# Expert blocks of a mixture of experts: 32x32 squares turned by VectorE in place of full transposes by TensorE

## What is computed

```python
D_MODEL = 1024
N_EXPERTS = 32
TOP_K = 2
D_EXPERT = 512
...
    def run_block(args):
        tok, gate, e = args
        xb = x_pad[tok]
        hdn = jax.nn.silu(xb @ wg[e]) * (xb @ wu[e])
        return (hdn @ wd[e]) * gate[:, None]
```

## Time and profile before

| | |
|---|---|
| median of 3 runs | 3002.2 us (2997.6 to 3004.9) |
| the profiled execution, first to last instruction | 3002.4 us |
| mean granted clock of TensorE in it | 0.969 of 2.4 GHz |
| TensorE busy | 2798.6 us (93%) |
| VectorE, ScalarE, GpSimd busy | 1423.0, 888.2, 416.7 us |
| bytes moved by DMA | 580.55 MB, mean 193 GB/s |
| loops over blocks (experts) | from about 2036 us to 2913 us |

### The profile page before, as it was taken

The page is one execution under the profiler, slowest core; times in us unless marked ns, Lnnn a source line. Parts: engine busy times, 40 slices in busy tenths (PEclk is TensorE's granted clock), DMA queues, the critical chain, the costliest instruction groups (busy, mean ns, idle before and its releaser), DMA issues. The chain is left out here.

```text
span 3002.4 us, 81057 instructions
## 1 busy us (share of the span) xinstructions
PE 2798.6 (93%) x33765; PEld 1640.7 (55%) x33766; DVE 1423.0 (47%) x3553; ACT 888.2 (30%) x1898; POOL 416.7 (14%) x633
## 2 busy tenths in 40 slices
PE   6998999999999989999998799958999999999988
PEld 3432445455454557887787455524555555555543
DVE  3246356555566647777777344561222222222218
ACT  2347244344344434444444122210000000000006
POOL 0000000000000001121123000003222222222223
PEclk8999999999999989999999799979999999999999
DMA  8641124223232396556553785555896588768858
GB/s 296 217 142 43 50 86 136 74 106 119 99 127 107 119 252 162 161 156 183 160 151 90 242 295 196 218 202 183 302 336 252 202 303 310 282 247 297 293 198 341
DMA packets 377451, 580.55 MB, mean 193 GB/s; under 512 B 56526, under 2 KB 240774, under 8 KB 374184
## 3 DMA queue, kind: packets, MB, share of 16 engines
q1 hardware_dynamic: 327176, 486.12, 47.2%
q0 software_dynamic: 18832, 70.53, 6.7%
q10 hardware_dynamic: 31248, 21.08, 2.4%
HBM read 412.03 MB, written 165.60 MB: 192 GB/s over the span
## 5 line engine op out<-in xcount | busy, mean ns | idle before, releaser
L523 PE MATMUL pj_P<-normed,pj_wc 128*128 128x448 f32 (+2 forms) x1600 | 594.8, 519 | 0.9 <-ACT pj_stage L656 0.9
L2714 PE MATMUL moe_PG<-wgu,moe_xT 128*32 128x256 f32 x9600 | 550.7, 381 | 0.0
L523 PEld LDWEIGHTS pj_P<-normed,pj_wc 128*128 128x128 f32 x1600 | 295.8, 190 | 259.5 <-issue 243.6
L2714 PEld LDWEIGHTS moe_PG<-wgu,moe_xT 128*32 128x32 f32 x9600 | 297.0, 110 | 206.6 <-issue 26.8
L2544 DVE TENSOR_TENSOR moe_sg<-moe_sg,moe_PG 128x128 f32<-128x128 f32 x150 | 43.1, 288 | 556.0 <-ACT moe_sg L2593 556.0
L2725 PE MATMUL moe_PTY<-wd,moe_hT 128*32 128x256 f32 x4800 | 286.5, 379 | 0.6 <-DVE moe_hT L2549 0.6
L2593 ACT ACTIVATE moe_sg<-moe_PG 128x128 f32<-128x128 f32 x150 | 41.8, 278 | 793.3 <-PE moe_PG L2714 793.3
L2132 PE MATMUL merge_PO<-merge_w,merge_mT 128*128 128x512 f32 x544 | 240.0, 599 | 0.6 <-ACT merge_mT L2178 0.6
L2725 PEld LDWEIGHTS moe_PTY<-wd,moe_hT 128*32 128x32 f32 x4800 | 155.9, 110 | 103.5 <-DVE moe_y L2537 0.7
L2132 PEld LDWEIGHTS merge_PO<-merge_w,merge_mT 128*128 128x128 f32 x544 | 102.7, 191 | 125.1 <-issue 124.4
L2636 POOL DMA_INDIRECT moe_xg<-scratch_h,moe_row x154 | 149.9, 974 | 125.7 <-POOL moe_xc L2649 114.9
(11 more groups left out here) (434 smaller groups left out, 4231.6 us busy)
## 6 DMA issues: line engine op xcount, KB each, us to landing
wgu<-in_w_gate SPq DMA_DIRECT2D x32, 2048.0 KB
wgu<-in_w_up SPq DMA_DIRECT2D x32, 2048.0 KB
wd<-in_w_down SPq DMA_DIRECT2D x32, 2048.0 KB
scratch_y_rows<-merge_zeros SPq DMA_DIRECT2D x51, 512.0 KB, 4.8
scratch_hk<-pj_hk SPq DMA_DIRECT2D x16, 1344.0 KB, 5.8
normed<-scratch_hk SPq DMA_DIRECT2D x32, 640.0 KB, 7.9
re_hkf<-scratch_hk SPq DMA_DIRECT2D x32, 640.0 KB
scratch_y_rows<-moe_y ACTq DMA_DIRECT2D x604, 32.0 KB
```

What stands on the lines that cost most here:

```text
L523: ins = eng.matmul(bank[:, 0:wp], wc[:, j, k, :], hT[:, k, k0:k0 + wp], start=(k == 0), stop=(k == KD - 1), skip_group_check=True)
L2714: ins = eng.matmul(PG[32 * q:32 * q + 32, 0, 0:256].rearrange("p (a b) -> p a b", a=2), x_rows, wgu[p][:, :, k, 128 * q:128 * q + 128], st ...
```

## The change

VectorE turns x and hid in squares of 32x32, each within its 32 partitions. `turn_x` reads a gathered buffer `xg` with every eighth element together and writes `xT` (128 partitions, 8 steps, 32 rows): partition 32q + i of step k then holds input 256q + 8i + k, that is 8p + k. `hT` is made in the same manner with 4 steps, input 4p + k. The weights are therefore loaded with rows (p k) in place of (k p). TensorE's `turn` and `turn_hid`, the PSUM tile `PT`, the buffer `xc`, GpSimd's copy and the copies out of PSUM by ScalarE and VectorE are gone. `gate_up` waits for `xT_made` and for `hid_ready`, since VectorE must have read the PSUM bank of the block before. GpSimd's next gather waits for `xT_made`.

```diff
@@ -1985,7 +1985,7 @@
 def load_expert(eng, t, e, gate_up, down, loaded, matrices=range(3)):
 
     for n in matrices:
-        src = t[("w_gate", "w_up", "w_down")[n]][0, ds(e, 1)].rearrange("e (k p) n -> p (e k) n", p=128)
+        src = t[("w_gate", "w_up", "w_down")[n]][0, ds(e, 1)].rearrange("e (p k) n -> p (e k) n", p=128)
         eng.dma_start(gate_up[:, n, :, :] if n < 2 else down[:, :, :], src).then_inc(loaded[n], 16)
 
 
@@ -2366,16 +2366,14 @@
         restart = sb("restart", [128, N_EXPERTS, NT])
 
         xg = [sb(f"xg{p}", [128, 256]) for p in range(2)]
-        xc = sb("xc", [128, 256])
-        xT = sb("xT", [128, 2, 128])
+        xT = sb("xT", [128, KD, BLOCK])
         sg = sb("sg", [128, 128])
         hid = sb("hid", [128, 128])
-        hT = sb("hT", [128, 128])
+        hT = sb("hT", [128, KE, BLOCK])
         y = [sb(f"y{p}", [128, 256]) for p in range(2)]
         PTY = ctx.enter_context(nc.psum_tensor("moe_PTY", [128, 2, 512], F32))
         PG = ctx.enter_context(nc.psum_tensor("moe_PG", [128, 2, 512], F32))
         PH = ctx.enter_context(nc.psum_tensor("moe_PH", [128, 2, 512], F32))
-        PT = PTY[:, 0, 0:256].rearrange("p (a b) -> p a b", b=128)
         PY = PTY[:, 1, 0:256]
         within = PG[:, :, :].rearrange("p a b -> p (a b)")[:, 0:NT * N_EXPERTS].rearrange("p (n e) -> p n e", e=N_EXPERTS)
         ident = const[:, 0, :]
@@ -2536,17 +2534,26 @@
                     eng.wait_ge(ev(f"y{p}_out"), stored * 64 + 64)
                     eng.tensor_copy(y[p][:, :], PY[:, :]).then_inc(ev("y_kept"), 1)
 
+                def turn_x(p):
+
+                    eng.transpose(xT[:, :, :], xg[p][:, :].rearrange("p (i k) -> p k i", k=KD)).then_inc(ev("xT_made"), 1)
+
+                eng.wait_ge(ev("gathered0"), 16)
+                turn_x(0)
                 n_pairs = total(eng) // 2
                 with eng.Fori(0, n_pairs) as i:
                     for p in range(2):
                         g = i * 2 + p
+                        eng.wait_ge(ev(f"gathered{1 - p}"), i * 16 + (16 + 16 * p))
+                        eng.wait_ge(ev("gu_made"), g + 1)
+                        turn_x(1 - p)
                         eng.wait_ge(ev("sigmoid_made"), g + 1)
                         eng.tensor_tensor(sg[:, :], sg[:, :], PG[:, 0, 0:128], ALU.mult).then_inc(ev("silu_made"), 1)
                         eng.wait_ge(ev("silu_made"), g + 1)
                         eng.tensor_tensor(hid[:, :], sg[:, :], PG[:, 0, 128:256], ALU.mult).then_inc(ev("hid_ready"), 1)
                         keep_y(g + 1, 1 - p, i)
-                        eng.wait_ge(ev("h_turned"), g + 1)
-                        eng.tensor_copy(hT[:, :], PH[:, 0, 0:128]).then_inc(ev("hT_kept"), 1)
+                        eng.wait_ge(ev("hid_ready"), g + 2)
+                        eng.transpose(hT[:, :, :], hid[:, :].rearrange("p (i k) -> p k i", k=KE)).then_inc(ev("hT_made"), 1)
                 keep_y(n_pairs * 2 + 1, 1, n_pairs)
 
                 def normalise(n):
@@ -2583,19 +2590,14 @@
                     eng.sem_inc(ev("store_begun"), 1)
 
                 n_blocks = total(eng)
-                eng.wait_ge(ev("x_turned"), 1 + 1)
-                eng.copy(xT[:, :, :], PT[:, :, :]).then_inc(ev("xT_kept"), 1)
                 n_pairs = n_blocks // 2
                 with eng.Fori(0, n_pairs) as i:
                     for p in range(2):
                         g = i * 2 + p
                         eng.wait_ge(ev("gu_made"), g + 1)
                         eng.activation(sg[:, :], PG[:, 0, 0:128], ACT.Sigmoid).then_inc(ev("sigmoid_made"), 1)
-                        eng.wait_ge(ev("x_turned"), g + 3)
-                        eng.copy(xT[:, :, :], PT[:, :, :]).then_inc(ev("xT_kept"), 1)
                         store_y(g, 1 - p)
                 store_y(n_pairs * 2, 1)
-                eng.wait_ge(ev("xT_kept"), n_pairs * 2 + 1)
                 eng.wait_ge(ev("y0_out"), n_pairs * 64 + 64)
                 eng.wait_ge(ev("y1_out"), n_pairs * 64 + 128)
                 eng.sem_inc(ev("all_stored"), 1)
@@ -2639,16 +2641,13 @@
                     eng.tensor_copy(row[:, p:p + 1], rows[:, p:p + 1]).then_inc(ev("row_ready"), 1)
                     eng.wait_ge(ev("row_ready"), p + 1)
                     gather(p)
-                n_pairs = (n_blocks + 2) // 2
+                n_pairs = n_blocks // 2
                 with eng.Fori(0, n_pairs) as i:
                     for p in range(2):
                         eng.wait_ge(ev(f"gathered{p}"), i * 16 + 16)
                         eng.tensor_copy(row[:, p:p + 1], rows[:, ds(i * 2 + (p + 2), 1)]).then_inc(ev("row_ready"), 1)
-                        eng.wait_ge(ev("x_turned"), i * 2 + (p + 1))
-                        eng.sem_inc(ev("move_begun"), 1)
-                        eng.tensor_copy(xc[:, :], xg[p][:, :]).then_inc(ev("x_moved"), 1)
                         eng.wait_ge(ev("row_ready"), i * 2 + (p + 3))
-                        eng.wait_ge(ev("x_moved"), i * 2 + (p + 1))
+                        eng.wait_ge(ev("xT_made"), i * 2 + (p + 1))
                         gather(p)
                 for p in range(2):
                     eng.wait_ge(ev(f"gathered{p}"), n_pairs * 16 + 16)
@@ -2667,7 +2666,7 @@
                 eng.wait_ge(ev("member_ready"), 1)
 
 
-                for name in ("x_turned", "y_made", "y_kept"):
+                for name in ("hid_ready", "y_made", "y_kept"):
                     eng.sem_inc(ev(name), 1)
                 for p in range(2):
                     eng.sem_inc(ev(f"y{p}_out"), 64)
@@ -2691,38 +2690,24 @@
                 eng.matmul(PG[:, 0, 0:MAX_BLOCKS + 1], quarters[:, :, :].rearrange("p a b -> p (a b)"), of_quarters[:, :], start=True, stop=True).then_inc(ev("rows_made"), 1)
                 eng.wait_ge(ev("rows_ready"), 1)
 
-                def turn(g, first=False):
-
-                    eng.wait_ge(ev("x_moved"), g + 1)
-                    if not first:
-                        eng.wait_ge(ev("xT_kept"), g)
-                    for k in range(2):
-                        ins = eng.transpose(PT[:, k, :], xc[:, 128 * k:128 * k + 128], ident)
-                    ins.then_inc(ev("x_turned"), 1)
-
-                def turn_hid(g):
-
+                def gate_up(g, p):
+
+                    eng.wait_ge(ev("xT_made"), g + 1)
                     eng.wait_ge(ev("hid_ready"), g + 1)
-                    eng.transpose(PH[:, 0, 0:128], hid[:, :], ident).then_inc(ev("h_turned"), 1)
-
-                def gate_up(g, p):
-
-                    eng.wait_ge(ev("xT_kept"), g + 1)
                     for k in range(KD):
-                        x_rows = xT[:, k % 2, 32 * (k // 2):32 * (k // 2) + 32]
                         for q in range(4):
-                            ins = eng.matmul(PG[32 * q:32 * q + 32, 0, 0:256].rearrange("p (a b) -> p a b", a=2), x_rows, wgu[p][:, :, k, 128 * q:128 * q + 128],
+                            ins = eng.matmul(PG[32 * q:32 * q + 32, 0, 0:256].rearrange("p (a b) -> p a b", a=2), xT[:, k, :], wgu[p][:, :, k, 128 * q:128 * q + 128],
                                              start=(k == 0), stop=(k == KD - 1))
                     ins.then_inc(ev("gu_made"), 1)
 
 
                 def down(g, p):
 
-                    eng.wait_ge(ev("hT_kept"), g)
+                    eng.wait_ge(ev("hT_made"), g)
                     eng.wait_ge(ev("y_kept"), g + 1)
                     for k in range(KE):
                         for n in range(4):
-                            ins = eng.matmul(PY[32 * n:32 * n + 32, :], hT[:, 32 * k:32 * k + 32], wd[p][:, k, 256 * n:256 * n + 256],
+                            ins = eng.matmul(PY[32 * n:32 * n + 32, :], hT[:, k, :], wd[p][:, k, 256 * n:256 * n + 256],
                                              start=(k == 0), stop=(k == KE - 1))
                     ins.then_inc(ev("y_made"), 1)
 
@@ -2730,8 +2715,6 @@
 
                     with eng.Fori(1, count) as b:
                         g = g0 + b
-                        turn(g + 1)
-                        turn_hid(g - 1)
                         gate_up(g, p)
                         down(g, p)
                         eng.nop()
@@ -2749,12 +2730,9 @@
                     eng.wait_ge(loaded[p][2], i * 16 + 16)
                     eng.sem_inc(ev("down_begun"), 1)
 
-                turn(0, first=True)
                 before, first, second = blocks_of_pair(eng, 0)
                 for matrix in range(3):
                     eng.wait_ge(loaded[0][matrix], 16)
-                eng.wait_ge(ev("xT_kept"), 1)
-                turn(1)
                 gate_up(before, 0)
                 rest_of_expert(before, first, 0)
                 next_expert(before + first, 0, 1)
@@ -2766,7 +2744,6 @@
                     next_expert(before + first, i, 1)
                     rest_of_expert(before + first, second, 1)
                 n_blocks = total(eng)
-                turn_hid(n_blocks - 1)
                 down(n_blocks, 1)
 
 
```

## The result

| | before | after |
| --- | --- | --- |
| median (range), us | 3000.18 (2997.6 to 3004.9) | **2957.61** (2952.99 to 2961.96) |
| profiled execution's span, us | 3002.4 | 2958.6 |
| expert stage, first gate/up to last group of down, us | 875.9 | 834.7 |

The ratio is 0.985 (95% interval 0.983 to 0.987), 42.6 us less. The forecast was 88 us less, 2915, with a range that ended at 2950: the direction was right, the time lies above the range, and half of the gain is missing. The stage gave 41.2 us and its start 1.7 us, so the missing half must be looked for in the stage.

What follows compares the result with a forecast made beforehand. TensorE was taken to bound the kernel, busy 872 of the stage's 876 us. Terms 90.3 - 4.4 - 1 + 3.0 = 87.9 us off 3002.4 gave 2914.5, forecast as 2915 us, range 2901 to 2950.

Steps and rivals of the forecast that it cites:

- TensorE, transposes out: Between down and the next gate/up: removing three full-width transposes saves 0.61 us at each of 148 boundaries, 90.3 us.
- rival (d): TensorE's hole before gate/up stays, since its own code is late: 19 us lost, 2934 us; chance 0.06.
- Turn of a pair: TensorE's fifteen reads of the next pair's block numbers: 0.62 us extra each instead of 0.33, 4.4 us back.
- VectorE, x: 128x256 transpose before the products making hid: 0.58 us, nothing lost; up to about 0.74 before TensorE waits.
- (a): VectorE transposes x square by square, 1.52 us, so TensorE waits: 3029 us, slower; chance 0.06.
- (b): VectorE's x transpose takes two passes, about 1.0 us, losing 38 us: 2953 us; chance 0.08.
- VectorE, hid: 128x128 transpose of hid, 0.3 to 0.8 us replacing a 0.29 copy; down needs it 3.5 us later: costs nothing.
- GpSimd: Its 0.4 us copy of gathered rows goes; gathers of 5.5 us fit in 9.8 with 4 to spare, unwaited.
- Start: First gate/up of the expert stage begins near 2033.5 instead of 2036.47, with one VectorE transpose: 3.0 us off.
- Weight loads: Weight DMAs in 16 KB runs should do no worse than shorter ones; 1 us lost for one late load.
- Rival (c): Weight loads become the bound, 16 KB runs bringing 330 GB/s instead of 380: 2937 us (to 2960); chance 0.10.

Runs made afterwards that it cites:

- e1: Changed kernel with each weight matrix loaded by two DMAs of every second row, so packets are 2 and 4 KB: 2916.29 us, ratio 0.972.
- e3: Changed kernel with each weight matrix loaded by two DMAs, each half of a partition's rows, so packets are 8 KB: 2912.95 us, ratio 0.970.
- e7: Changed kernel, 16 KB packets kept, with three of the four store DMAs of y left out: 2911.65 us, ratio 0.970.
- e8: Changed kernel with 8 KB packets, VectorE's turn of x reading its columns densely instead of every eighth element: 2912.95 us, ratio 0.971.
- e12: Changed kernel, 16 KB packets kept, with four store DMAs a block of 8 rows each in place of 32: 2911.04 us, ratio 0.970.
- e5: Changed kernel, 16 KB packets kept, storing a block's y by one DMA of 128 KB in place of four of 32 KB: 3164.19 us, ratio 1.054.
- e4: Kernel before the change, old transposes kept, with only the weight loads changed to rows (p k), giving 16 KB packets: 3002.61 us, ratio 1.000.
- e6: Changed kernel, 16 KB packets kept, with each weight matrix loaded by two DMAs of 64 partitions each: 3420.89 us, ratio 1.140.

## Why the prediction was wrong, and where it was right

- **TensorE, transposes out: right.** 0.61 us a boundary were forecast, to a period of 5.18. The period is reached: in e1, e3, e7, e8 and e12 115 to 132 of the 149 periods are within 0.05 us of it, and nearly all of the rest are over by less than 0.3 us or lie at the turn of a pair. The hole went with the transposes, so rival (d) falls. With packets of 8 KB the stage is 84.4 us shorter than before (875.9 - 791.5), where its terms gave 90.3 - 4.4 - 1 = 84.9: of the terms of the stage all stand but one, the loads. That the whole kernel then takes 2912.95 us, 2 us from the 2915 of the sum, is in part luck, since its start moved too, by more than the change can do (below).
- **Turn of a pair: right.** 0.62 us of extra each was taken. In e3 the starts of gate/up behind the fifteen loads of the table come 9.4 us late in all, 0.63 each.
- **VectorE, x: right in kind, short in size.** 0.58 us was taken, 0.653 measured; the strided read costs 0.21 instead of 0.16, the dense part 0.445 instead of 0.42. It stays under the 0.74 at which TensorE would wait, so rivals (a) and (b) fall.
- **VectorE, hid: right.** 0.413 us, within 0.3 to 0.8, and not on the path, unless the copy of y ahead of it waits for a store (e5).
- **GpSimd: right in cost, wrong in a sign.** Gathers were to be "unwaited", and GpSimd waits for them for 82.0 us. But the x turn hardly does (6.2 us in two waits), and e7 shows that they cost nothing.
- **Start: 3.0 us forecast, 1.7 measured.** Gate/up begin at 2034.78 instead of 2036.47. The first gather was issued at 2031.21, 1.5 us later than in the profile before (2029.66), in a part that the change does not touch; from there to the first gate/up it is 3.6 us instead of 6.8, so the two rounds of copy and turn went as forecast. In the profiles of the further runs of the changed kernel the first gather comes anywhere from 2021.3 to 2045.1 us, in e3 at 2022.6, 7 us ahead of before: the start of the stage is known no better than that.
- **Weight loads: the step that failed.** "Longer runs should do no worse" was argued from the weights' own rate, and of that it is true: 26.8 GB/s an engine, and no engine waits for a matrix. What was not costed is what a 611 ns packet does to the *other* queues. The prediction went through gathers, weights and the copy of y, and never through the wait that stands ahead of that copy, on the store two blocks back, though `keep_y` names it. The rows to do it with were there: a store's time under 2 KB packets is in the trace of before (6.4 us), and an estimate of eight packets on each engine times half a microsecond more would have given over 10 us against a slack of 8.7. The term for the loads was 1 us; what the long packets cost measured 44.7 (2957.61 - 2912.95), some 42 of it in the block periods, and e7 and e12 put it down to the stores of y.
- **Rival (c)** had the words for it, "gathers and stores held up behind long packets", with a chance of 0.10 and a time of 2937 to 2960. The time fits and the mechanism is not the one it was priced by: it took the delay as a lower rate of the weights, at short experts. The weights were on time; it was the latency of a small transfer, in every block beside a load. A rival that is priced by the wrong quantity could not show that it needed a larger chance. Its "only 4% of DMA is spare" is not in its row either: the earlier trace rows has a DMA share of 1.02, with nothing to spare.

What stays open: whether the 15 turns of a pair (9.4 us) could be hidden by reading the table earlier was not tried. Nor was a third y buffer, which by the same arithmetic should make 16 KB packets harmless (15.5 us less 1.65, room for 10.8).

## What to carry to other kernels

When you make a DMA's contiguous runs longer, ask not only what rate it will have but who shares its engines: a small transfer spread over the engines was delayed here by about (its packets on each engine) x (length of one foreign packet), on top of the 6.1 us that it took beside the shortest packets, and the whole must fit the reuse distance of its buffer. Here 8 KB runs kept the rate and cost nothing, and cutting each load in two, a few lines, is worth 45 us over the change as made: 2912.95 us, 0.970 of the kernel before, is the version to keep. And when a schedule is tightened, walk every wait in the loop against the new period, the ones that never waited before included; late stores cost nothing at 5.8 us a block (e4) and 45 us at 5.18.

## What the runs showed that was not expected

- A packet of 16384 bytes takes 611 ns, of 8192 bytes 309, of 4096 bytes 159, of 2048 bytes 84. From 8 KB to 16 KB the rate of an engine hardly grows (26.5 to 26.8 GB/s).
- Two loads of 64 partitions each in place of one of 128 run at half the rate: 1202 ns a packet, 212 GB/s at a DMA share of 0.94 (e6).
- One DMA whose outermost dimension on one side is 4 has 4 completions in place of 16, and takes 17.2 us under load in place of 10.8 for four DMAs with the same bytes (e5).
- Beside any full stream of weights the first packet of a store comes 3.5 to 4.4 us after its issue, with none 0.8 to 1.3.
- VectorE turns 128x256 f32 as 32x32 squares in 445 ns when it reads densely, 653 at a stride of eight elements, and 128x128 at a stride of four in 413.
